# Small products of a four-layer block in quarter tiles of TensorE, both depthwise convolutions as products, and a reordered passage and odd layer end

## What is computed

```python
for l in range(DEPTH):
    h = layer_norm(ALPHA * h + 0.5 * swiglu_ffn(h, ffn1...), ...)
    h = layer_norm(ALPHA * h + token_mix(h, w_in[l], ...), ...)
    h = layer_norm(ALPHA * h + 0.5 * swiglu_ffn(h, ffn2...), ...)
```

## Time and profile before

| | |
|---|---|
| runs | 1777.63 us median of 3 (1777.48 to 1779.65) |
| the profiled execution's own time | 1778.24 us |
| its span | 1776.3 us, mean granted TensorE clock 0.981 |
| PE busy | 1696.2 us, 95% of the span |
| DVE, ACT, POOL busy | 1167.0, 812.7, 237.9 us |
| DMA | 279.57 MB, mean 157 GB/s |
| layer 0's mixer | about 238 to 337 us; layer 1's 774 to 873 |
| passage to the second block | 1084 to 1106 us |
| odd layer's end and projection | 1534 to 1569 us |

### The profile page before, as it was taken

How to read it: one execution, slowest core, us unless ns; L and a number is a source line. 1 busy time by engine, 2 the same in 40 slices (tenths; PEclk the granted TensorE clock), 3 DMA queues, 4 the chain that set the end, 5 groups by cost and what they waited for, 6 DMA issues and landing times.

```text
span 1776.3 us, 31965 instructions
## 1 busy us (share of the span) xinstructions
PE 1696.2 (95%) x13256; PEld 1645.0 (93%) x13256; DVE 1167.0 (66%) x1590; ACT 812.7 (46%) x1058; POOL 237.9 (13%) x212
## 2 busy tenths in 40 slices
PE   7999999999999999999999996999999999889998
PEld 6999999899999999998899995988999998889997
DVE  5556597686556755587586645566866578677664
ACT  5333473563335433373563434663434355354343
POOL 1002400310032001400220041221100020020000
PEclk9999999999999999999999998998999999999998
DMA  5455443344544555443355552342455533144551
GB/s 209 165 181 186 166 151 119 119 166 166 196 178 152 175 177 187 167 153 119 120 191 185 196 194 92 126 149 98 144 186 209 191 121 107 64 144 175 186 210 74
DMA packets 37298, 279.57 MB, mean 157 GB/s; under 512 B 4320, under 2 KB 4448, under 8 KB 7120
## 3 DMA queue, kind: packets, MB, share of 16 engines
q1 hardware_dynamic: 35440, 269.63, 42.7%
q0 software_dynamic: 1760, 8.56, 1.4%
HBM read 277.13 MB, written 1.05 MB: 157 GB/s over the span
## 4 chain that ended last, share of the span: by engine, by line
PE 76%; DVE 10%; ACT 8%; issue 3%; DMA 1%; POOL 1%; SPq 0%; ACTq 0%; DVEq 0%; POOLq 0%
PE bank L712 24%; PE bank L714 23%; PE bank L713 23%; ACT w_hi L1458 4%; DVE w_lo L2087 4%; DMA raw<-in_up_w 1%; ACT h L1522 1%; ACT h_hi L1521 1%; PE bank L1071 1%; POOL h L648 1%; PE bank L1096 0%; PE bank L1023 0%; PE bank L1256 0%; PE bank L1321 0%; DVE win L2519 0%
## 5 line engine op out<-in xcount | busy, mean ns | idle before, releaser
L2087 DVE TENSOR_TENSOR w_lo<-raw,w_hi 128x2048 fp32r<-128x2048 f32 (+4 forms) x235 | 576.1, 2452 | 278.3 <-ACT w_hi L1458 278.1
L712 PE MATMUL bank<-h_hi,w_hi 128*128 128x256 f32 (+1 forms) x2304 | 663.8, 288 | 20.7 <-DVE h_lo L2243 10.0
L714 PE MATMUL bank<-h_hi,w_lo 128*128 128x256 f32 (+1 forms) x2304 | 660.1, 287 | 0.0
L713 PE MATMUL bank<-h_lo,w_hi 128*128 128x256 f32 (+1 forms) x2304 | 658.7, 286 | 0.0
L1458 ACT ACTIVATE w_hi<-raw 128x2048 fp32r<-128x2048 f32 (+3 forms) x238 | 477.2, 2005 | 314.2 <-PE bank L714 185.3
L712 PEld LDWEIGHTS bank<-h_hi,w_hi 128*128 128x128 f32 x2304 | 438.1, 190 | 27.3 <-issue 16.3
L714 PEld LDWEIGHTS bank<-h_hi,w_lo 128*128 128x128 f32 x2304 | 438.0, 190 | 0.0
L713 PEld LDWEIGHTS bank<-h_lo,w_hi 128*128 128x128 f32 x2304 | 437.1, 190 | 0.1
L712 PE MATMUL bank<-g_hi,w_hi 128*128 128x256 f32 (+1 forms) x1312 | 377.9, 288 | 15.9 <-DVE y L2295 4.0
L714 PE MATMUL bank<-g_hi,w_lo 128*128 128x256 f32 (+1 forms) x1312 | 373.1, 284 | 0.0
L713 PE MATMUL bank<-g_lo,w_hi 128*128 128x256 f32 (+1 forms) x1312 | 372.9, 284 | 0.0
(11 more groups left out here) (371 smaller groups left out, 1894.6 us busy)
## 6 DMA issues: line engine op xcount, KB each, us to landing
raw<-in_up_w SPq DMA_DIRECT2D x111, 1024.0 KB, 4.8
raw<-in_down_w SPq DMA_DIRECT2D x48, 1408.0 KB, 5.8
raw<-in_in_w SPq DMA_DIRECT2D x20, 1024.0 KB, 4.8
raw<-in_up_w SPq DMA_DIRECT2D x16, 1152.0 KB, 5.1
raw<-in_out_w SPq DMA_DIRECT2D x16, 1024.0 KB, 4.8
raw<-in_even_w SPq DMA_DIRECT2D x12, 1024.0 KB, 4.8
raw<-in_odd_w SPq DMA_DIRECT2D x6, 1024.0 KB, 4.8
diag<-in_conv_w POOLq DMA_DIRECT2D x4, 1024.0 KB, 5.1
```

What stands on the lines that cost most here:

```text
L712: pe.matmul(out, w[0], x[0], start=first, stop=False)
L713: pe.matmul(out, w[0], x[1], start=False, stop=False)
L714: return pe.matmul(out, w[1], x[0], start=False, stop=last)
L2087: last = dve.tensor_tensor(lo[:, b:n], raw[:, slot, b:n], hi[:, b:n].bitcast(F32), ALU.subtract)
```

## The change

1. Both halves of the convolution on PE, after chunk 5. Four taps and 32 channels make the 128 rows of a product, 32 channels its columns; four such products go to the four groups of 32 columns of a bank, eight steps accumulate. The moving operand `u4` holds the padded input four times, shifted by 0 to 3; SP fills it by 16 DMAs from SBUF to SBUF behind the load of chunk 6. DVE's taps go; POOL loads one diagonal tile.
2. The last 32 tokens of the value chunks, and the gate tile, are no longer made by `mm3` but by 8 plain float32 products from `raw`, in four column groups (two products accumulate in each). The four partial sums are left on four groups of partitions and added by the products that use them, which now take 128 rows; the last keys are copied four times for that. The loads that would overwrite `raw` wait (`raw_used`).
3. Variances of the four heads: one product each with 32 equal columns, in the four column groups of one bank; root and reciprocal over 128 x 272; four products of 32 rows spread them, after chunk 11. The pointwise products move to c = 9, the split of y's first four tiles on DVE to c = 10.
4. ACT splits chunk 6 before chunk 4's copies, DVE within the pool windows.
5. The passage: the split of even chunk 1 moves behind the norm, DVE works on pairs of tiles, gain and bias go into ACT's squares, and h is written after the squares.
6. The odd layer's end: two tiles of `project_first` before the last `by_feature`, two behind it; ACT's split before the last `high_part`; `true_residual` behind the copies.

```diff
-TAP_HALF = 16
+ROWS = 32
+TAP_ROWS = 4
+TAP_STEPS = -(-TAPS // TAP_ROWS)
+TAP_COLS = P // TAP_ROWS
+U4 = T + TAP_ROWS * (TAP_STEPS - 1)
 KTOK = [(0, 128), (128, 128), (256, 16)]
...
-        diag = place("diag", [P, TAP_HALF, P], offset=sq_at)
-        few = placer(region((sq_at + TAP_HALF * P * 4, sq_at + KD * T4)))
-        o_std = few("o_std", [P, 3 * HEADS])
-        o_inv1 = few("o_inv1", [P, 3 * HEADS])
-        v_sum = few("v_sum", [P, 2, 2, 2])
-        v_sum2 = few("v_sum2", [P, 2, 2])
...
+            def shifted_taps(l):
+                sp.wait_ge(conv_in, l + 1)
+                for r in range(TAP_ROWS):
+                    for g in range(TAP_ROWS):
+                        sp.dma_start(u4[TAP_COLS * r:TAP_COLS * (r + 1), :, g, :],
+                                     upad[TAP_COLS * g:TAP_COLS * (g + 1), :, r:r + U4]).then_inc(taps_loaded, 16)
+            def straight(chunks, raw_use=lambda i: 0, mixed=None):
...
+                straight([(a["in_w"][l, c, :, 0:n * KD * P], n * KD) for c, n in enumerate(IN_GROUPS)],
+                         lambda c: 2 * l + c - 8 if c in (9, 10) else 0, l)
...
+                     lambda c: 2 * LAYERS + 1 if c == 5 else 0)
...
-                pool.dma_start(diag[:], a["conv_w"][l, 0]).then_inc(diag_loaded, 16)
-                pool.wait_ge(diag_used, l + 1)
-                pool.dma_start(diag[:], a["conv_w"][l, 1]).then_inc(diag_loaded, 16)
+                pool.dma_start(diag[:], a["conv_w"][l]).then_inc(diag_loaded, 16)
...
+            def last_tokens(bank, slot):
+                for half in range(2):
+                    for g in range(4):
+                        k = 4 * half + g
+                        last = pe.matmul(bank[TAIL * g:TAIL * (g + 1), 0:2 * P], h[:, k, T - TAIL:],
+                                         raw[:, slot, 2 * k * P:(2 * k + 2) * P], start=half == 0, stop=half == 1)
+                last.then_inc(raw_used, 1)
+            def gate_tile(bank, slot, tiles, e):
+                for half in range(2):
+                    for g in range(4):
+                        k = 4 * half + g
+                        col = (k * tiles + e) * P
+                        last = pe.matmul(bank[TAIL * g:TAIL * (g + 1), 0:S], raw[:, slot, col:col + TAIL], y[:, k, 0:S],
+                                         start=half == 0, stop=half == 1)
+                return last
...
+                def conv_taps():
+                    pe.wait_ge(diag_loaded, (l + 1) * 16)
+                    pe.wait_ge(taps_loaded, (l + 1) * 16 * TAP_ROWS ** 2)
+                    for j in range(2):
+                        for i in range(TAP_STEPS):
+                            for g in range(TAP_ROWS):
+                                last = pe.matmul(ps[4 + j][TAP_COLS * g:TAP_COLS * (g + 1), 0:T], diag[:, j, g, i, :],
+                                                 u4[:, j, g, TAP_ROWS * i:TAP_ROWS * i + T],
+                                                 start=i == 0, stop=i == TAP_STEPS - 1)
+                        last.then_inc(conv_mm, 1)
...
-                        last = pe.matmul(ps[7][0:m, hd * n:(hd + 1) * n], kT[:, hd, lo:lo + m],
+                        last = pe.matmul(ps[7][:, hd * n:(hd + 1) * n], k_tail(hd // 2)[:, hd % 2 * P:(hd % 2 + 1) * P],
...
-                    for t, (lo, m) in enumerate(KTOK):
-                        last = pe.matmul(ps[VALUE_BANKS[hd]][:, SEEN_FROM[t]:T], v_tok[0:m, t, hd * P:(hd + 1) * P],
-                                         pT[0:m, hd, SEEN_AT[t]:SEEN_AT[t] + T - SEEN_FROM[t]],
+                    for t in range(3):
+                        last = pe.matmul(ps[VALUE_BANKS[hd]][:, SEEN_FROM[t]:T], v_tok[:, t, hd * P:(hd + 1) * P],
+                                         pT[:, hd, SEEN_AT[t]:SEEN_AT[t] + T - SEEN_FROM[t]],
...
-                    for t, (lo, m) in enumerate(KTOK):
-                        for hd in range(HEADS):
-                            col = t * HEADS + hd
-                            last = pe.matmul(ps[1][0:m, col:col + 1], o_sq[:, hd, lo:lo + m], ones[:, 0:1],
-                                             start=True, stop=True)
+                    for hd in range(HEADS):
+                        last = pe.matmul(ps[2][ROWS * hd:ROWS * (hd + 1), 0:T], ones[:, 0:ROWS], o_sq[:, hd, :],
+                                         start=True, stop=True)
...
+                def scale_rows():
+                    pe.wait_ge(ret_inv, seen.next(ret_inv))
+                    pe.wait_ge(ret_y, seen.at(ret_y, 3))
+                    for hd in range(HEADS):
+                        rows = slice(ROWS * hd, ROWS * (hd + 1))
+                        last = pe.matmul(ps[SCALE_BANKS[hd]][:, 0:T], ones[rows, :], rstd[rows, :], start=True, stop=True)
                     last.then_inc(ret_b, 1)
...
-                    elif c == 10:
-                        variances()
                         pe.wait_ge(conv_act, seen.next(conv_act, 2))
-                        for j, b in enumerate((2, 5)):
+                        for j, b in enumerate((1, 5)):
                             for k in range(2):
                                 last = pe.matmul(ps[b][:, 0:T], mixw[:, 2 + 2 * k + j, :], conv_y[:, k, :],
                                                  start=k == 0, stop=k == 1)
                             last.then_inc(conv_pwd, 1)
-                        pe.wait_ge(ret_inv, seen.next(ret_inv))
-                        for hd in range(HEADS):
-                            scale_row(hd)
-                        seen.skip(ret_y, HEADS)
+                    elif c == 10:
+                        variances()
+                        pe.wait_ge(small_done, seen.next(small_done, 2))
+                    elif c == 11:
+                        pe.wait_ge(z_copied, seen.at(z_copied, 21))
+                        scale_rows()
 
                 in_tiles(IN_GROUPS, IN_ORDER, VALUES, [m for _, m in KTOK], 4, z_copied, T, mixers, DEFER)
                 if l == LAYERS - 1:
                     first.lo = META
-                pe.wait_ge(small_done, seen.next(small_done, 2))
                 project_first(range(4))
                 pe.wait_ge(z_copied, seen.next(z_copied, 22))
                 project_first(range(4, KD))
...
-            project_first(range(4), S, None)
+            project_first(range(2), S, None)
             by_feature(1, 1)
+            project_first(range(2, 4), S, None)
...
-                    if c and not (shifted and c <= shifted + 1):
+                    if shifted and c == shifted + 1:
+                        split_next(sizes[c + 2] * KD, 0, c + 2)
+                    elif c and not (shifted and c <= shifted + 2):
...
+                    if c == CONV_AT + 1:
+                        for j in range(2):
+                            act.wait_ge(conv_mm, seen.next(conv_mm))
+                            act.activation(conv_y[:, j, :], ps[4 + j][:, 0:T], ACT.Identity, bias=vcol(l, V_CDB + j))\
+                                .then_inc(conv_done, 1)
...
+                    act.activation(std[:], ps[2][:, 0:T], ACT.Sqrt, scale=ROWS ** 2 / P, bias=eps[:, 3:4])\
+                        .then_inc(ret_std, 1)
...
             for k in range(KD):
-                act.wait_ge(normed, seen.next(normed))
-                act.activation(xk(k), y[:, k, META:T], ACT.Identity, bias=vcol(LAYERS - 1, V_LN + 40 + k))\
-                    .then_inc(x0_ready, 1)
+                if k % 2 == 0:
+                    act.wait_ge(t_ready, seen.next(t_ready))
+                act.activation(sq[:, k, 0:S], y[:, k, META:T], ACT.Square, **last_norm(k)).then_inc(squared, 1)
+            for k in range(KD):
+                act.activation(xk(k), y[:, k, META:T], ACT.Identity, **last_norm(k)).then_inc(x0_ready, 1)
 
...
-                    if n < T and restore and c < 2:
-                        true_residual(c)
...
+                    if restore and c < 2:
+                        true_residual(c)
...
+                        if i == 2:
+                            split_next(IN_GROUPS[DEFER + 3] * KD, 0, DEFER + 3)
...
+                    dve.reciprocal(rstd[:], std[:]).then_inc(ret_inv, 1)
...
+                    if c == 6:
+                        dve.wait_ge(rope_ready, l * (2 * HEADS + 1) + 2 * HEADS)
+                        for j in range(2):
+                            keys = kT[:, 2 * j:2 * j + 2, T - TAIL:].rearrange("p h (a n) -> p h a n", a=1)
+                            last = dve.tensor_copy(k_tail(j).rearrange("p (h a n) -> p h a n", h=2, n=TAIL),
+                                                   keys.broadcast_to([P, 2, TAIL_COPIES, TAIL]))
+                        last.then_inc(rope_ready, 1)
...
-                assert tap == TAPS
                 for hd in range(3):
                     scaled_head(hd)
-                if l == LAYERS - 1:
-                    first.lo = META
-                mix_split(range(7), T)
                 gated_head(3)
                 scaled_head(3)
```

(16 more changed lines are left out.)

188 lines of the change are left out of this document (82 added, 106 removed).

## The result

| | before | changed |
|---|---|---|
| runs | 1778.63 us median of 4 (1777.48 to 1779.65) | 1750.88 us median of 4 (1748.35 to 1752.89) |
| ratio | | 0.9844, interval 0.983 to 0.9858 |
| profiled execution's span | 1776.3 | 1746.5, mean granted clock 0.979 |

A forecast was written before the change was run, and what follows sets the result against it. PE, busy for 95% of the span, was taken as the bound. Gains of 30 (both mixers), 4.7 (passage), 1.8 (even layer) and 6.5 (odd end) made 43: 1777.6 - 43 = 1735 us, range 1725 to 1749.

The forecast's parts named there:

- I take four: Quarter tiles: products in four groups of 32 columns run four at a time; convolution 7.3 + 0.3 us, gain 6.6 per layer.
- Rivals 2 and 3: Quarter tiles: only two column groups run at a time, 1756 us (8%); or one after another, about 1797 us (5%).
- The gather: Mixer, before the convolution: PE, free at 257.6, waits for 16 DMAs landed at 258.2; cost 0.7 us per layer.
- rival 1: Mixer: the gather lands 3 to 6 us after 258.2, each us costing 2; 1741 to 1747 us, chance 12%.
- SP issues one per 0.465 us: Step for the gather's 16 DMAs on SP's queue: at that spacing the last is issued at 255.9 us.
- The clock in the mixers: Forecast had no term for it; clock terms only at the passage and in the odd layer (2.2 us there).
- The end's waits: Mixer's end: PE waits 0.5 for the reciprocal and 1.4 for the first output chunk's low part; cost 1.9 per layer.
- gain 0.9: Mixer's end: PE's 1.63 us wait for y, DVE being busy with a split, shrinks to about 0.75.
- The sum per layer: All mixer terms together gain 14.7 us, say 15 per layer, 30 for both.
- The passage: Passage to the second block: PE starts 5.6 us sooner relative to the mean, the root 4.2 to 5.2; gain 4.7.
- The even layer: Gate tile's 24 passes, 2.8 us, become 1.15 with PE busy throughout; full rows save 0.15; gain 1.8.
- The odd end: Odd layer's end: waits 1.4 and 4.6 us shorter, clock gives 2.2; gain 6.5, or 4 if the clock falls.

The follow-up runs named there:

- whole rows: Changed kernel with the gather's same bytes sent by four transfers of 128 partitions each, so the convolution's values differ: 1741.2 us, ratio 0.9788.
- three queues: Changed kernel with the sixteen gather transfers issued by SP (eight), ACT (four) and POOL (four) instead of SP alone: 1748.5 us, ratio 0.9823.
- gate tile full: Changed kernel with the even layer's gate tile made as before, by 24 full products, its second product from 16 rows: 1752.1 us, ratio 0.9846.
- odd end old: Changed kernel with the odd layer's end as before (PE's order, ACT's split, the restoring on DVE): 1756.5 us, ratio 0.9872.

## Why the prediction was wrong

- **Side by side** (step "I take four"): right, 0.056 us per pass. 7.54 us for the convolution, forecast 7.6. Tails, values, variances and scale rows: right to 0.13 us each. Rivals 2 and 3 fell. What the third describes, one pass after another, comes back with the other order of the loops (0.229 within a group); the forecast didn't name the order as its condition, and the change happened to have the right one.
- **The gather** (cost 0.7): this failed. It is rival 1 in kind (chance 12%), with a delay of 2.4 us where that rival had 3 to 6, and the forecast's own sign of being wrong, a wait over 3 us inside the mixer, came. The step "SP issues one per 0.465 us" took a row of other transfers; these take 0.67. The last was issued at 258.4 and not at 255.9; PE went on 2.2 later, so the landing time of 2.0 was about right. Cost 3.3 and 4.1: 2.6 and 3.4 us per layer more than the term, 6.0 in all. That a us of this wait costs a us in each layer is right: with whole rows the wait is 2.5 shorter and chunk 6 starts 2.5 sooner.
- **The clock in the mixers**: this failed, and no rival had it. The forecast reckoned with the clock at the passage and in the odd layer, where the trace before showed falls, and nowhere else. But it itself put in waits that the mixer hadn't had: 0.5 and 1.4 at its end (measured 0.40 and 1.45) and one at the gather, and priced what the clock does behind them at nothing, without a reason. Three falls of 1.5 and one of 1.7 make 6.2 us.
- **The end's waits** (1.9 per layer, less 0.9 for y): the first was right. The wait for y went from 1.63 to 0.25, but the next grew by 1.4, to 1.86: the term "gain 0.9" is nil.
- **The sum per layer**: 14.7 forecast for layer 0, less 2.6 (gather), 3.0 (two falls) and 0.9 (y), makes 8.2; measured 9.2. Layer 1: 14.7 - 3.4 - 3.2 - 0.9 = 7.2; measured 8.4. The 1.0 and 1.2 beyond are small: about 0.3 is the products' own, 0.3 a wait for conv_y that went (the forecast had counted it as 0); the rest I haven't traced.
- **The passage** (4.7): 4.4, by its own steps but three. PE started 5.9 us sooner against its last sums (forecast 5.6). ACT's squares with gain and bias take 0.51 and not 0.41 (in the trace before, a square with neither takes 0.32 and the writing of h with a bias alone 0.41), and the writing of h ended at 1079.9, 0.9 after PE's sums, so h held up the root. As the clock is 0.50 for 6.8 us behind it and not 3.4, chunk 0 then gives 0.5 back.
- **The even layer** (1.8): 0.7 behind chunk 0, in keeping with the 0.6 that undoing it costs. The gate tile's 1.9 us on PE came, but POOL's first normalised tile, until then hidden, is late by 1.33. The step said "with PE busy throughout that stretch" and never asked who else has to be ready sooner.
- **The odd end** (6.5): 7 between the traces, 6.2 when undone. Right.

15.2 us are missing between the forecast gain and that of the medians. 12.2 are the gather and the clock, 1.8 the term for y in both layers, 1.9 the passage and the even layer, 0.6 the rounding of 14.7 to 15; 2.2 of small gains in the mixers and 0.6 at the odd end go the other way, and so does 0.5 by which the profile was ahead before the mixers. That makes 13.2; the other 2 are the profiled execution, which was the quickest of the four.

## What to carry to other kernels

Work taken off the engine that bounds brings forward the moment at which all others must be ready: walk once more along each stretch that gets shorter and ask what ended just in time (here the gather, DVE's rotations and POOL's tile; each became a wait of 1.3 to 4.1 us). Price a new wait of TensorE twice, for itself and for the clock that may fall behind it; where it can't be removed, idle products into a bank that will be overwritten are worth trying. Where two limits lie on each other, take both away in one run before you decide which it was.

## What the runs showed of the hardware that I had not expected

- The order in which products of different column groups are queued decides: 0.056 us per pass in turn, 0.229 between neighbours of one group, with the same work and clock.
- A transfer of 75 KB from SBUF to SBUF on 32 partitions costs SP 0.67 us to issue in the changed kernel (0.90 when three queues issue at once, single ones up to 1.92), one of 300 KB on 128 partitions 0.74. A packet of 1,200 bytes took 89 ns in the first, 71 in the second and 53 in the third.
- Waits of 0.40 and 1.45 us, 1.9 in all and 2.2 us apart, were followed by 3.41 us at 1.2 GHz in both layers of the changed kernel; single ones of 1.0 and 1.6 in the kernel before were not. The same wait isn't always followed by a fall. The one of 3.33 us at layer 0's gather wasn't in the changed kernel, while in two runs with the same code up to there (gate tile full, 3.27, and odd end old, 3.23) it was; and the pair of 0.40 and 1.45 in layer 0 wasn't in the run with the gate tile full. That is a part of the runs' spread (1748.35 to 1752.89).
